# Diffusion layer step on one core: the modulation product for groups 2 to 11 moved from TensorE to VectorE, its weights loaded on GpSimd's queue

## The reference

```python
def modulation(cond, w_ada, b_ada):
    m = jax.nn.silu(cond) @ w_ada + b_ada
    return jnp.split(m[:, None, :], N_MOD, axis=-1)      # N_MOD = 6 vectors of 1024

def trunk_layer(x, cond, ...):
    shift1, scale1, gate1, shift2, scale2, gate2 = modulation(cond, w_ada_l, b_ada_l)
    h = rms_norm(x, g_mix) * (1 + scale1) + shift1
    mo, k, v = mixer(h, w_in_l, ...)
    x = x + gate1 * mo
    h = rms_norm(x, g_ffn) * (1 + scale2) + shift2
    x = x + gate2 * ffn(h)
```

## Time and profile before

| what | value |
|---|---|
| median of 3 runs | 1874.77 us (1870.79 to 1877.24) |
| the profiled execution | 1868.69 us, its span 1866.8 us |
| TensorE matmul (PE) busy | 1808.4 us, 97% |
| VectorE (DVE) busy | 1112.9 us, 60% |
| ScalarE (ACT) busy | 788.4 us, 42% |
| GpSimd (POOL) busy | 137.5 us, 7% |
| DMA | 290.54 MB, mean 156 GB/s |

### The profile page before, as it was taken

One profiled execution on the slowest core, in us unless ns is written; L12 is line 12 of the kernel. 1 busy time (PEld: TensorE's weight loads), 2 busy tenths in 40 slices (PEclk: granted clock), 3 DMA queues, 4 the chain that ended last, 5 costly groups with the idle time before them and its releaser, 6 DMA issues.

```text
span 1866.8 us, 30905 instructions
## 1 busy us (share of the span) xinstructions
PE 1808.4 (97%) x12352; PEld 1678.5 (90%) x12352; DVE 1112.9 (60%) x1909; ACT 788.4 (42%) x1334; POOL 137.5 (7%) x108
## 2 busy tenths in 40 slices
PE   7999989999999999999999889999999999999997
PEld 6999857999999999999999669898989989999886
DVE  2644686544442344345635884476877778778787
ACT  4222265432221222233221464274656657666575
POOL 2000000200000000011000001222000000002221
PEclk8999999999999999999999999999999999999999
DMA  9435200322423223232245000296877768778972
GB/s 367 156 122 215 68 1 1 136 102 102 144 72 124 102 102 140 76 124 107 97 159 168 25 1 24 79 248 217 256 261 242 270 224 279 262 240 296 317 226 72
DMA packets 93845, 290.54 MB, mean 156 GB/s; under 512 B 15368, under 2 KB 23944, under 8 KB 93696
## 3 DMA queue, kind: packets, MB, share of 16 engines
q1 hardware_dynamic: 86784, 271.20, 42.8%
q0 software_dynamic: 6912, 17.30, 2.8%
HBM read 281.98 MB, written 12.28 MB: 158 GB/s over the span
## 4 chain that ended last, share of the span: by engine, by line
PE 90%; DVE 5%; ACT 1%; issue 1%; DMA 1%; SPq 0%; POOL 0%; POOLq 0%; ACTq 0%; DVEq 0%
PE ps L781 49%; PE ps L1150 12%; PE ps L1173 6%; PE ps L1151 5%; PE ps L1183 4%; PE ps L847 3%; PE ps L976 2%; PE ps L922 2%; PE ps L1154 2%; PE ps L1161 2%; DVE nbias L2110 1%; PE ps L1153 1%; DVE pr L2127 1%; PE ps L1265 1%; DMA ada_raw<-ada_w 1%
## 5 line engine op out<-in xcount | busy, mean ns | idle before, releaser
L1952 DVE TENSOR_TENSOR w_lo<-raw,w_hi 128x1024 fp32r<-128x1024 f32 x394 | 481.9, 1225 | 343.5 <-ACT w_hi L1388 335.5
L1388 ACT ACTIVATE w_hi<-raw 128x1024 fp32r<-128x1024 f32 x394 | 414.1, 1053 | 313.6 <-PE ps L781 171.3
L1150 PE MATMUL ps<-hg,w_hi 128*128 128x320 f32 (+5 forms) x1232 | 347.1, 351 | 2.3 <-DVE w_lo L1952 2.3
L781 PE MATMUL ps<-a_hi,w_hi 128*128 128x320 f32 x1472 | 341.4, 313 | 3.4 <-DVE a_lo L1983 3.4
L781 PE MATMUL ps<-a_hi,w_lo 128*128 128x320 f32 x1472 | 336.5, 310 | 0.0
L781 PE MATMUL ps<-a_lo,w_hi 128*128 128x320 f32 x1472 | 333.6, 307 | 0.0
L1151 PE MATMUL ps<-hg,w_lo 128*128 128x160 f32 (+5 forms) x1232 | 300.7, 244 | 0.0
L781 PEld LDWEIGHTS ps<-a_hi,w_hi 128*128 128x128 f32 x1472 | 247.0, 188 | 12.1 <-issue 8.1
L781 PEld LDWEIGHTS ps<-a_lo,w_hi 128*128 128x128 f32 x1472 | 248.5, 188 | 0.0
L781 PEld LDWEIGHTS ps<-a_hi,w_lo 128*128 128x128 f32 x1472 | 245.0, 188 | 0.0
L1150 PEld LDWEIGHTS ps<-hg,w_hi 128*128 128x128 f32 x1232 | 233.0, 189 | 3.5 <-DVE w_lo L1952 3.0
(11 more groups left out here) (322 smaller groups left out, 2579.1 us busy)
## 6 DMA issues: line engine op xcount, KB each, us to landing
raw<-gu_w SPq DMA_DIRECT2D x220, 512.0 KB, 4.6
raw<-moe_down_w SPq DMA_DIRECT2D x88, 512.0 KB, 4.4
ada_raw<-ada_w SPq DMA_DIRECT2D x21, 2048.0 KB, 8.4
raw<-in_w SPq DMA_DIRECT2D x48, 512.0 KB, 9.6
raw<-down_w SPq DMA_DIRECT2D x22, 512.0 KB, 3.4
raw<-out_w SPq DMA_DIRECT2D x16, 512.0 KB, 3.5
ada_pro<-ada_w SPq DMA_DIRECT2D x2, 2048.0 KB, 18.5
y_rows<-ey POOLq DMA_DIRECT2D x7, 512.0 KB
```

Of the source, the lines that this page charges most:

```text
L781: ins = nc.tensor.matmul(out[:, hf, 0:c1 - c0], w, o[:, c0:c1], start=f, stop=e)
L1150: nc.tensor.matmul(sums, whi, both, start=(k == 0), stop=False)
L1388: nc.scalar.activation(w_hi[:, s, :], raw[:, n % RAW, :], ACT.Copy).then_inc(hi_done, 1)
L1952: nc.vector.tensor_tensor(w_lo[:, s, :], raw[:, n % RAW, :], w_hi[:, s, :].bitcast(F32), ALU.subtract)\
```

## The change

For groups 2 to 11 the product is no longer TensorE's. VectorE multiplies each chunk of 128 x 1024 weights by a per-partition condition value and adds it to one of two accumulators of 128 x 1024 (`weigh_modulation`, once for each condition). TensorE only sums the 128 partitions of the two accumulators with a column of ones (`sum_conditions`, 8 matmuls for a group in place of 32). Groups 9 to 11 move from layer 1's in stage into the dense mixer. The chunks come singly on GpSimd's queue into two halves of the old tile, and the 20 loads of 2 MB leave SP's queue.

```diff
+def mingle(items, groups, counts, allowed):
...
+        for g, k in WEIGHED[items[i]]:
+            if k == KB - 1:
+                spots = [j for j in range(i + 1, len(items)) if allowed(j)]
+                at.setdefault(spots[0], []).append(("ada", "rows", g, 0))
+                at.setdefault(spots[1], []).append(("ada", "turn", g, 0))
...
+def unit_counts(u, i):
+    if i < 2 * FB - 2:
+        return 0 if u == 0 and i < 2 else 2 if i in ((4, 8, 10, 14, 16, 18), (2, 6, 10, 14))[u] else 1
+    return int(u == 0 and 2 * FB <= UNIT[i][0] < 2 * FB + KB and UNIT[i][2])
...
-IN_SEQ[0] = mingle(IN_SEQ[0], range(2, 5), lambda i: i > 0)
-IN_SEQ[1] = mingle(IN_SEQ[1], range(9, 12), lambda i: i > 0)
+IN_COUNTS = {"k": (0, 1, 1, 1), "q": (1, 1, 1, 1), "v": (2, 1, 2, 1), "gc": (1, 1, 1, 1), "xin": (2, 1, 2, 1),
+             "gb": (1, 0, 0, 0), "turn": (0, 0, 0, 0)}
+IN_SEQ[0] = mingle(IN_SEQ[0], range(2, 5), [IN_COUNTS[_kind][_j] for _kind, _j in IN_SEQ[0]], lambda i: True)
...
+            def sum_conditions(grp, g):
+
+                pe.wait_ge(ada_done, KB * (grp - 1))
+                for c in range(2):
+                    for j in range(4):
+                        ins = nc.tensor.matmul(ps[32 * j:32 * j + 2, g % 4, 0, 0:QCOLS], pick[:, 1 - c:3 - c],
+                                               ada_acc[:, c, j * QCOLS:(j + 1) * QCOLS], start=c == 0, stop=c == 1)
+                ins.then_inc(mm_done, 1)
...
+            def load_modulation(groups):
+
+                for grp in groups:
+                    for k in range(KB):
+                        m = KB * (grp - 2) + k
...
+                            pool.wait_ge(ada_done, m - 1)
+                        nc.gpsimd.dma_start(ada_raw[:, m % 2, :], ada_w[grp // 6, KB * (grp % 6) + k])\
+                            .then_inc(ada_in[m % 2], 16)
...
+            def weigh_modulation(item):
+
+                for grp, k in WEIGHED[item]:
+                    m = KB * (grp - 2) + k
+                    dve.wait_ge(ada_in[m % 2], 16 * (m // 2 + 1))
+                    if m:
+                        dve.wait_ge(ada_done, m)
+                    if k == 0 and grp > 2:
+                        dve.wait_ge(mm_done, ROWS_AT[grp - 3] + 1)
+                    for c in range(2):
+                        part, share = ada_raw[:, m % 2, :], cs[:, k, c:c + 1]
+                        if k == 0:
+                            ins = nc.vector.tensor_scalar(ada_acc[:, c, :], part, share, None, ALU.mult)
+                        else:
+                            ins = nc.vector.scalar_tensor_tensor(ada_acc[:, c, :], part, share, ada_acc[:, c, :],
+                                                                 op0=ALU.mult, op1=ALU.add)
+                    ins.then_inc(ada_done, 1)
```

More of the change, by code:

```diff
@@ L151 @@
              ("turn", 0, 0): 0, ("rows", 1, 1): 2, ("turn", 1, 0): 2}
[L154 to L163, removed]
+WEIGHED = {}
+def mingle(items, groups, counts, allowed):
+    steps = [(g, k) for g in groups for k in range(KB)]
+    at, done = {}, 0
+    for i, count in enumerate(counts):
+        WEIGHED[items[i]] = steps[done:done + count]
+        done += count
+        for g, k in WEIGHED[items[i]]:
[3 more added lines that the diff above has]
+                at.setdefault(spots[1], []).append(("ada", "turn", g, 0))
+    assert done == len(steps)
     out = []
@@ L168, in mingle @@
     return out
-DENSE = mingle([("unit", u, i) for u in range(2) for i in range(len(UNIT))], range(5, 9),
-               lambda i: i > 1 and i % len(UNIT) < 2 * FB)
+def unit_counts(u, i):
+    if i < 2 * FB - 2:
+        return 0 if u == 0 and i < 2 else 2 if i in ((4, 8, 10, 14, 16, 18), (2, 6, 10, 14))[u] else 1
+    return int(u == 0 and 2 * FB <= UNIT[i][0] < 2 * FB + KB and UNIT[i][2])
+UNIT_ITEMS = [(_u, _i) for _u in range(2) for _i in range(len(UNIT))]
+DENSE = mingle([("unit", _u, _i) for _u, _i in UNIT_ITEMS], range(5, 12), [unit_counts(_u, _i) for _u, _i in UNIT_ITEMS],
+               lambda i: i % len(UNIT) < 2 * FB)
 IN_KINDS = [("k", j) for j in range(4)] + [("q", j) for j in range(4)] + [("v", j) for j in range(4)] \
@@ L469, in hybrid_step @@
         ada_full = sem("ada_full")
+        ada_in = [sem(f"ada_in{i}") for i in range(2)]
+        ada_done = sem("ada_done")
         pro_full = [sem(f"pro_full{i}") for i in range(4)]
@@ L652, in _ @@
                         load_cache(l)
[L653 to L656, removed]
+                    if c is not None:
                         load(n, in_w[l, w])
@@ L905, in _ @@
                             turn_rows(g, grp + 1, grp)
-                    u = 1
                 def scores(*ms):
@@ L938, in _ @@
                             open_block(g0 + b)
[L939 to L941 removed]
+                            sum_conditions(item[2], g0 + b)
                         continue
@@ L2042, in modulation_item @@
             def modulation_item(item, g, q):
-                _, kind, grp, q_ = item
+                _, kind, grp, _ = item
                 if kind == "turn":
@@ L2076, in _ @@
             nc.vector.memset(cs[:], 0.0).then_inc(cs_clear, 1)
+            for i in range(3):
+                nc.vector.memset(pick[:, i:i + 1], float(i == 1))
             dve.wait_ge(consts_in, 16 * 3)
@@ L2147, in _ @@
                         free_spread(2 * l)
+                    if l == 0:
+                        weigh_modulation(item)
                     slot, done = (g0 + b) % 4, IN_CH * l + c + 1
```

32 lines of the change are left out of this document (16 added, 16 removed).

## The result

The changed kernel takes 1886.68 us (median of 4 runs, 1882.86 to 1888.01), the kernel before on the same chip 1873.57 us. The ratio is 1.0068, with a 95% interval of 1.0051 to 1.0085: 10 to 16 us slower. The profiled execution took 1886.57 us.

What follows compares the result with a forecast made beforehand. TensorE, with 90% of the chain of waits, was taken to bound the kernel. New waits of 36 us against a gain of 30.9 made +5 us, 1880 us from the median of 1874.77; range 1858 to 1900.

Steps and rivals of the forecast that it cites:

- What TensorE is rid of: Twenty rows items of 2.07 us go, ten new ones of 1.05 come: 30.9 us gained in both in stages and dense mixer.
- The third rival: The new rows items on TensorE don't run side by side: 31 us more, 1911 us; chance 0.05.
- What VectorE is given: Seventy chunks at 2.42 us and ten at 1.4: 183 us, by totals within VectorE's 343 us of spare time.
- Waits in the dense mixer: Weighing lengthens the chain of VectorE and ScalarE to 7.3 us against TensorE's 7.04; TensorE waits 18.5 us in all.
- shared item: Dense mixer item weighing one group's last chunk and the next's first: VectorE starts late, TensorE waits 4.0 us at the turn.
- Waits in the in stage: Layer 0's in stage: steps of 8.5 us with a weighed chunk against TensorE's 7.04; TensorE waits 17.7 us in all.
- The loads: Chunks of 512 KB on GpSimd's queue, wanted 7.3 us after weighing at the earliest; no cost taken.
- The second rival: Loads come late behind the 14 items with two chunks: 1892 us, or 1903 at 9 us; chance 0.13.
- The first rival: VectorE's 183 us hide in its 343 us of spare time and the 30.9 us gain stays: 1844 us; chance 0.22.

Runs made afterwards that it cites:

- e9: Changed kernel, but groups 2 to 4 stay in layer 0's in stage as before, and the dense mixer weighs behind the output scaling: 1859.61 us, ratio 0.9929.
- e9b: As e9, but weighing ahead of the output scaling, as in the changed kernel: 1877.37 us, ratio 1.0025.
- e1: Changed kernel with weighing moved behind the output scaling for gate and up chunks and in the in stage: 1869.46 us, ratio 0.9981.
- e10: e9 with other counts, so that no dense item weighs for two groups: 1855.01 us, ratio 0.9910; once more 1852.69 us, 0.9887.
- e6: e1 with other counts, so that no item weighs for two groups: 1871.31 us, ratio 0.9996.
- e3: Changed kernel with matmuls whose result nothing reads ahead of the turns of groups 2, 5, 6 and 9: 1884.59 us, ratio 1.0064.
- e11: e6 with the in stage's chunks spread by room, fewer under k and q, none under v0: 1860.28 us, ratio 0.9931.
- e2: Changed kernel with the turn of seven groups one chunk later: 1883.8 us, ratio 1.0062.
- e4_half: Changed kernel with each chunk weighed for one condition only, TensorE summing the same accumulator twice: 1863.73 us, ratio 0.9949.

## Why the prediction came out as it did

The changed kernel is slower for the reason given: the weighing stands between the split and the output and lengthens a chain of two engines, and the waits cost more than the matmuls saved. For the dense mixer this is shown: e9 and e9b differ in that order alone, -2.9 us against +13.8, and e1 against the changed kernel says the same. For the in stage it is shown that the weighing makes the loss (e9, +0.2 without it), but not that its place does, since e1's order gives back only 0.8 us there. What the profile shows of that stage is that VectorE takes 8.48 us for a k step, 1.09 of them waiting for ScalarE's bias, and has no gap ahead of the next output (below). The time fell 7 us above the 1880 forecast, and I go through the terms.

**What TensorE is rid of.** A new rows item lasts 1.04 us and costs 508.75 - 506.97 - 0.59 = 1.19, not 1.05, since the pair behind it starts late:

```profile
506.97 0.46 PE L789 MATMUL ps<-a_hi,w_lo 128*128 128x320 f32 x2
507.36 1.04 PE L865 MATMUL ps<-ada_raw,pick 128*2 128x256 f32 x16
508.33 0.58 PE L789 MATMUL ps<-a_hi,w_hi 128*128 128x320 f32 x2
508.75 0.45 PE L789 MATMUL ps<-a_lo,w_hi 128*128 128x320 f32 x2
```

The gain is 29.5 us in place of 30.9. Where no wait is left it shows in full: layer 1's in stage is 13.9 us shorter (six rows items and three turns, 6 x 2.07 + 3 x 0.45 = 13.8), and the dense mixer in e10 6.5 (8 x 2.07 - 7 x 1.19 - 3 x 0.45 = 6.9). The third rival, rows items that don't run side by side, is out.

**What VectorE is given.** 1279 and 749 ns against 1282 and the chosen 750. Right.

**Waits in the dense mixer.** Forecast 18.5 us, measured 12.6. The three turns behind a shared item wait 4.04, 4.04 and 4.03, forecast 4.0, and e6 and e10 show that the shared item makes them. Group 5's rows item waits 0.50, forecast 0.6. The 5.9 us forecast for groups 6, 7, 10 and 11 outside those turns aren't there, because the slow clock ahead of them gave VectorE the time. In e3, where the clock stays up, 4.0 of them are: the rows items of groups 6, 7 and 10 wait 0.71, 2.28 and 0.71 against 1.2, 2.4 and 1.7, and group 11's turn waits 0.25 against 0.6.

**Waits in the in stage.** Forecast 17.7 us, measured 13.8. The k step with a weighed chunk is 82.75 - 74.27 = 8.48 us, forecast 8.5:

```profile
74.27 0.15 DVE L2029 TENSOR_REDUCE bcol<-ps 128x2 f32<-128x4 f32 x1
...
80.36 2.47 DVE L2096 SCALAR_TENSOR_TENSOR ada_raw<-ada_raw,cs 128x1024 f32<-128x1024 f32 x2
82.75 0.15 DVE L2029 TENSOR_REDUCE bcol<-ps 128x2 f32<-128x4 f32 x1
```

The five waits for `w_lo` are 0.23, 1.16, 1.38, 1.38 and 1.37 (forecast 0.2 to 1.8), group 2 waits 3.85 and 3.02 (forecast 4.0 and 3.7), group 3 1.39 (forecast 3.4). Here too the slow clock had come first: in e3, where it stays up behind group 2's turn, group 3 waits 2.93.

**The missing term: the clock.** This is the step that failed. The prediction priced a wait of TensorE at its own length. The three long waits of the dense mixer cost 7.7 us more by the slow clock, and the in stage has two stretches of it (granted 0.66 in 125 to 130 us, 0.67 in 140 to 145), (0.34 + 0.33) x 5 = 3.4 us. Terms for both stages: gain -7.9 - 9.3, waits +12.6 + 13.8, the dearer rows items +1.4, the clock +11.1, sum +21.7, against 11.2 + 14.2 = 25.4 measured. With layer 1's -13.9 in place of the forecast 12.4 + 1.35 the whole comes to +7.8 against +11.5. The other 3.7 us are in no term: 0.9 of it is a new wait at the first score (L938 for VectorE, none in before), 0.9 the slow clock at the in stage's start, which isn't the change's, and 1.9 weren't taken apart. So the waits forecast too high (10 us) and the clock left out (11) cancelled. In part that is no accident, as e3 shows that the slow clock itself takes waits away, but the sum didn't know it. The forecast was nearer than its terms deserved.

The page "TensorE: Matmul & The Clock Gate" of the Trainium skill, section "HAM oscillation — how this bites in real kernels", says that matmuls behind a long idle gap run at half rate. The rows at 469 us agree (pairs 0.54 us apart in place of 0.29), and the gap there costs 2.4 us. The prediction should have drawn on it.

**The loads.** 512 KB on GpSimd's queue land in 3.8 us, and VectorE never waits for them in the changed kernel. In the other kernels it does so twice, 0.58 us in e9 (503.8 us) and 1.17 in e11 (133.6 us). The second rival is out. Page "SBUF — State Buffer" of the Trainium skill, section "Who interferes with whom", has VectorE's two-port operations block GpSimd's descriptors. No run here shows that: the two slowest of the 80 landings, 6.8 and 8.4 us, are those of the first two loads (38.1 and 38.7 us), and no other took over 5.5.

**The first rival**, a hidden VectorE: not in this order. In e10's it comes true in the dense mixer, where the spare time was 269 us and where 6.5 us of a gain of 6.9 are kept. In the in stage, where totals gave 74 us for 21 x 2.42 + 3 x 1.4 = 55 of work, no order tried here did it.

## What to carry to other kernels

Work given to an engine with spare time should stand behind the step that another engine waits for: here the same 56 chunks make the dense mixer 14 us longer ahead of the output scaling, 2.9 shorter behind it, and 6.5 shorter with no shared item as well. When a stage reads better and the whole doesn't, make a table by stage and change one stage alone. A wait that is moved (e2) or filled (e3) comes back at the next place, so look for what makes the engine late, and price a long wait of TensorE at its length and the slow clock behind it.

## What the runs showed of the hardware

How long TensorE idles doesn't by itself say whether the granted clock falls. At rows items, turns and waits for `w_lo` it stayed up after every wait of 0.2 to 1.5 us and fell after every one of 3.85 us and more. In between it went both ways: it fell after 1.97 and 2.17 us (e4_half), 2.93 (e3_fill, 172 us), 3.02 (after, 139 us), 3.17 (e6_late_counts, 221 us) and 3.26 (e2_turn_later, 741 us), and stayed at 1.00 after 2.28 (e3_fill, 550 us), 2.67 (e2_turn_later, 503 us) and 3.23 (e1_late_weigh, 168 us). In e4_half it fell only 1.7 us behind the wait's end, while matmuls were running closely again:

```profile
452.74 0.61 PE L879 MATMUL ps<-fold,pT 128*128 128x8 f32 x4 [2.17 <-DVEq L2080]
...
454.16 0.51 PE L789 MATMUL ps<-a_hi,w_hi 128*128 128x320 f32 x2
454.47 0.73 PE L789 MATMUL ps<-a_lo,w_hi 128*128 128x320 f32 x2
455.00 0.74 PE L789 MATMUL ps<-a_hi,w_lo 128*128 128x320 f32 x2
```

What decides between 2.0 and 3.2 us is open. That this slow time is partly given back, since the engine that is late catches up in it (e3), I hadn't expected either.
